# Twelve pairs of seven-product tiles: weight sums on VectorE instead of GpSimd, first products copied ahead of rounding, and half a values tile inside the last mLSTM unit

## The chip, the cores and the metric

One core of a Trainium2 chip runs the whole program. The metric is device time in microseconds (us) of one execution; smaller is better. The engines that matter here are TensorE (PE in the profile; its weight loads are PEld), VectorE (DVE), ScalarE (ACT), GpSimd (POOL) and SyncE (SP), which issues the loads.

## The reference

One layer of a trunk, for 128 context tokens and 512 latent tokens (640 columns in all) of width 1024:

```python
h = rms_norm(x, n_pre[0]) * (1 + sc0) + sh0
x = x + 0.5 * g0 * rms_norm(swiglu(h, f_in[0], f_out[0]), n_post[0])     # FFN 0, D_FF = 2816
h = rms_norm(x, n_pre[1]) * (1 + sc1) + sh1
y, st = token_mixer(h, *mix_w, ctx)          # mLSTM (8 heads) beside grouped attention (16 heads)
x = x + g1 * rms_norm(y, n_post[1])
h = rms_norm(x, n_pre[2]) * (1 + sc2) + sh2
x = x + 0.5 * g2 * rms_norm(swiglu(h, f_in[1], f_out[1]), n_post[2])     # FFN 1

def swiglu(h, w_in, w_out):
    a, b = jnp.split(h @ w_in, 2, axis=-1)
    return (jax.nn.silu(a) * b) @ w_out
```

## The kernel before

**Products in three passes.** Everything lies transposed, features on the 128 partitions and the 640 tokens along a row. Each float32 operand is split into a rounded high part and a low remainder, and a product is three matmuls: high by high, high by low, low by high. A weight tile (128 output features, 1024 inputs) is loaded into one of four buffers `raw`. ScalarE rounds it into `whi`, VectorE subtracts and leaves `wlo`, and TensorE then runs 8 blocks of inputs by 2 halves of 320 columns by 3 passes, 48 matmuls (`project`, L646 to L648).

**FFN 1 with seven products.** The inner features of an FFN are done in three phases of 8, 8 and 6. In phase 1 of the second FFN all 8 gate and up tile pairs, and in phase 2 the first 4, go through `seven`: Strassen's scheme in Winograd's form on 2 x 2 blocks. The blocks of weights are the two halves of the inputs of the gate tile (`gt`) and of the up tile (`ut`); the blocks of tokens are the two halves of 320 columns. Seven products of 4 input blocks by 3 passes, 12 matmuls each, take the place of eight. I call a pair g (0 to 11; n is its number in its phase) and its products M0 to M6 (the code's `i`). They go into three banks of PSUM, A B A C B C B in this order, so that a bank is written again before the pair is over, and its content has to be taken away first:

- M2 overwrites M0 in bank A: ScalarE first copies it to `kept_p1` (L1252).
- M4 overwrites M1 in bank B: VectorE first makes `sum_u2` from it (L1865).
- M5 overwrites M3 in bank C: ScalarE first copies it to `kept_p5` (L1261).
- M6 overwrites M4 in bank B: VectorE first makes `sum_u3` (L1875).

Each product needs its own weights: M0, M2 and M6 take half a tile as loaded, and M1, M3, M4 and M5 take one of the sums `w_sum` 1, 0, 2 and 3, 128 x 512 each. ScalarE rounds each (`prod_high`, L1233, which I call H0 to H6), VectorE leaves the remainder (`prod_low`, L1833, L0 to L6), and both go into a ring of four half buffers, so that H of one product waits for the product four before it. GpSimd makes the four sums of a pair during the pair before it (`weight_sums`, L1782 to L1791).

At the end of the pair VectorE adds the up half and multiplies it by the gate after Silu (`pair_product`, L1845 and L1849); ScalarE rounds this into `g_hi` (L1244), and VectorE leaves `g_lo` (L1853). Both do so during the next pair. Silu itself is done in two halves on ScalarE: left (L1257) after VectorE's L1869, and right (L1270) after VectorE's L1888.

Every engine runs its instructions in the order of the code and stops at a wait until the semaphore is reached; nothing overtakes it. On ScalarE the order in a pair is H3, `g_hi` of the pair before, `kept_p1`, H4, H5, H6, Silu left, `kept_p5`, H0 and H1 of the next pair, Silu right, H2 of the next pair.

**mLSTM units.** After the state updates there are 20 units (`UNITS`). For each unit n TensorE makes the numerators (`nums_of`, L1003 and L1006) in banks 0 and 1, from which VectorE makes the outputs (L2379 to L2393), ScalarE the root mean square (L1577 to L1582), VectorE scales (L2398), TensorE turns the result (`turn_hm`, L1014) and ScalarE stores it (L1591). `nums_of(n)` waits until VectorE has read the banks for unit n - 1 (L2388). Between the small products of the units, halves of gate projection tiles (`half_gemm`, 24 matmuls each) are laid as filler. The last unit has none: its numerators follow on `turn_hm(17)`, then `turn_hm(18)`, then the whole tile of the values projection `gemm(L_AV)`, then `turn_hm(19)`.

Of the kernel before, what the change touches and what calls it, by code (L numbers as in the profile page):

```python
# [47 lines left out]
RAWS = 4  # L48
# [86 lines left out]
def build(nc, a):  # L135
    ctx = ExitStack()
    with ctx:
# [466 lines left out]
        def _(pe):  # L604
            mm, tp = pe.matmul, pe.transpose

            def seven(g, n, base):
                gt, ut = pair_tiles(base, n)
                for i in range(7):
                    if i < 5:  # L610
                        pe.wait_ge(prod_lo, KEEP + 5 * g + i + 1)
                    else:
                        pe.wait_ge(raw_free, (gt, ut)[i - 5].n + 1 + RAWS)
                    if i == 0:
                        pe.wait_ge(ev[ut.slot], ut.pair - 1)
                    if i == 1 and g == 0:
                        pe.wait_ge(tok_lo, KEEP + 4)
                    if i == 2:
                        pe.wait_ge(act_kept, KEEP + 4 * g + 1)
                    if i == 4:  # L620
                        pe.wait_ge(dve_sums, KEEP + 6 * g + 1)
                    if i == 5:
                        pe.wait_ge(act_kept, KEEP + 4 * g + 3)
                    if i == 6:
                        pe.wait_ge(dve_sums, KEEP + 6 * g + 3)
                    out = psum[:, pair_banks(n)[(0, 1, 0, 2, 1, 2, 1)[i]], 0:HALF]
                    (wh, wl), (th, tl) = product(g, i), of_tokens(i)
                    for k in range(KH):
                        mm(out, wh[:, k, :], th[:, k, :], start=(k == 0), stop=False)  # L629
                        mm(out, wh[:, k, :], tl[:, k, :], start=False, stop=False)  # L630
                        last = mm(out, wl[:, k, :], th[:, k, :], start=False, stop=(k == KH - 1))  # L631
                    last.then_inc(prod_done if i < 5 else tile_done, 1)
# [387 lines left out]
            for n in range(UNITS):  # L1020
                if n + 1 < UNITS:
                    half_gemm(10 + 2 * n)
                    spread_m(n + 1)
                    front_of(n + 1)
                    half_gemm(11 + 2 * n)
                nums_of(n)
                if n >= 1:
                    turn_hm(n - 1)
            gemm(L_AV)
            turn_hm(UNITS - 1)  # L1030

            def qk_stats(n):
# [177 lines left out]
        def _(act):  # L1210
# [24 lines left out]
            def seven(g, n, base, last, first_g):  # L1235
                gt, ut = pair_tiles(base, n)
                s = gt.c // 2 % 2
                bank_a, _, bank_c = (psum[:, b, 0:HALF] for b in pair_banks(n))
                left, right = HCOLS

                def pair_high(m, before):
                    up = pair_tiles(base, m)[1]
                    act.wait_ge(ev[up.slot], up.pair + 1)
                    copy(g_hi[:, m, :], sb[before][:, :]).then_inc(g_hi_s, 1)  # L1244

                prod_high(g, 3, n, base)
                if n:
                    pair_high(n - 1, 1 - s)
                act.wait_ge(prod_done, KEEP + 5 * g + 1)
                if g:  # L1250
                    act.wait_ge(dve_sums, KEEP + 6 * (g - 1) + 2)
                copy(kept_p1, bank_a).then_inc(act_kept, 1)  # L1252
                prod_high(g, 4, n, base)
                prod_high(g, 5, n, base)
                prod_high(g, 6, n, base)
                act.wait_ge(dve_sums, KEEP + 6 * g + 2)
                fn(sa[s][:, left], sa[s][:, left], ACT.Silu).then_inc(act_kept, 1)  # L1257
                act.wait_ge(prod_done, KEEP + 5 * g + 4)
                if g:
                    act.wait_ge(dve_sums, KEEP + 6 * (g - 1) + 5)  # L1260
                copy(kept_p5, bank_c).then_inc(act_kept, 1)  # L1261
                if not last:
                    prod_high(g + 1, 0, n + 1, base)
                    prod_high(g + 1, 1, n + 1, base)
                else:
                    t = Tile(base + 2 * n + 2)
                    act.wait_ge(prod_done, KEEP + 5 * g + 5)
                    split(t, None, 0, first_g)
                act.wait_ge(dve_sums, KEEP + 6 * g + 6)
                fn(sa[s][:, right], sa[s][:, right], ACT.Silu).then_inc(act_kept, 1)  # L1270
                if not last:
                    prod_high(g + 1, 2, n + 1, base)
                else:
                    split(Tile(base + 2 * n + 3), None, ut.n + 3, first_g)
                    pair_high(n, s)

# [459 lines left out]
        def _(pool):  # L1736
# [34 lines left out]
                step(8, t4, of_h(h_hi, down, left), t2[:, :, :], sub)  # L1771
                step(9, t4, of_h(h_lo, down, left), t4[:, :, :], ALU.add)

            def weight_sums(g, n, base):
                gt, ut = pair_tiles(base, n)
                a1, a2 = raw[gt.raw], raw[ut.raw]
                sub = ALU.subtract
                for t in (gt, ut):
                    pool.wait_ge(raw_in[t.raw], 16 * (t.quad + 1))
                if g:  # L1780
                    pool.wait_ge(prod_lo, KEEP + 5 * (g - 1) + 4)
                pool.tensor_tensor(w_sum[0][:, :, :], a2[:, 0:KH, :], a2[:, KH:KC, :], ALU.add).then_inc(w_sum_in, 1)  # L1782
                pool.wait_ge(w_sum_in, KEEP + 4 * g + 1)
                pool.tensor_tensor(w_sum[1][:, :, :], w_sum[0][:, :, :], a1[:, 0:KH, :], sub).then_inc(w_sum_in, 1)
                if g:
                    pool.wait_ge(prod_lo, KEEP + 5 * (g - 1) + 5)
                pool.tensor_tensor(w_sum[2][:, :, :], a1[:, 0:KH, :], a2[:, 0:KH, :], sub).then_inc(w_sum_in, 1)
                if n:
                    pool.wait_ge(raw_free, pair_tiles(base, n - 1)[0].n + 1 + RAWS)
                pool.wait_ge(w_sum_in, KEEP + 4 * g + 2)  # L1790
                pool.tensor_tensor(w_sum[3][:, :, :], a1[:, KH:KC, :], w_sum[1][:, :, :], sub).then_inc(w_sum_in, 1)  # L1791

            for l in range(3):
                if l == 2:
                    token_sums()
                    base = T_FFN1
                    for p, nj in enumerate(PHASES):
                        for n in range(SEVEN[p]):
                            weight_sums(SEVEN_FROM[p] + n, n, base)
                        base += 2 * nj + KC  # L1800
                if l == 0:
                    pool.wait_ge(h_rdy, KC)
                elif l == 1:
                    pool.wait_ge(yl, KC)
                else:
                    pool.wait_ge(h_rdy, KC + n_half(l - 1, 1, KC - 1))
                for h in range(2):
                    for i in range(1, KC - 1):
                        add_y_square(l, i, h)

        @block.vector
        def _(dve):
# [13 lines left out]
            def prod_low(g, i, n, base):  # L1826
                gt, ut = pair_tiles(base, n)
                if i < 5:
                    dve.wait_ge(prod_hi, KEEP + 5 * g + i + 1)
                else:  # L1830
                    dve.wait_ge(w_hi, (gt, ut)[i - 5].n + 1)
                hi, lo = product(g, i)
                tt(lo, of_weights(i, gt, ut), hi.bitcast(F32), ALU.subtract).then_inc(prod_lo if i < 5 else raw_free, 1)  # L1833

            def seven(g, n, base, last, first_g, first_j):
                gt, ut = pair_tiles(base, n)
# [32 lines left out]
                tt(sa[s][:, left], bank_a, kept_p1, ALU.add).then_inc(dve_sums, 1)  # L1869
                prod_low(g, 6, n, base)  # L1870
                if not last:
                    prod_low(g + 1, 0, n + 1, base)
                dve.wait_ge(prod_done, KEEP + 5 * g + 5)
                dve.wait_ge(dve_sums, KEEP + 6 * g + 1)
                tt(sum_u3, bank_b, sum_u2, ALU.add).then_inc(dve_sums, 1)  # L1875
                dve.wait_ge(act_kept, KEEP + 4 * g + 3)
                dve.wait_ge(dve_sums, KEEP + 6 * g + 3)
                if n >= 2:
                    dve.wait_ge(g_lo_s, first_j + n - 1)
# [8 lines left out]
                tt(sa[s][:, right], bank_c, sa[s][:, right], ALU.add).then_inc(dve_sums, 1)  # L1888
                if not last:
                    prod_low(g + 1, 2, n + 1, base)  # L1890
                else:
                    pair_product(n, s)
                    pair_low(n, s)
# [234 lines left out]
            def ffn(f, base):  # L2128
                it = j0 = 0
                for p, nj in enumerate(PHASES):  # L2130
# [60 lines left out]
                    elif f == 1:  # L2191
                        for m in range(KC):
                            t = Tile(base + m)
                            if m < KC - 2:
                                split(t.plus(2))
                            if m == KC - 2:
                                prod_low(SEVEN_FROM[p + 1], 0, 0, base + KC)
                                prod_low(SEVEN_FROM[p + 1], 1, 0, base + KC)
                            elif m == KC - 1:
                                prod_low(SEVEN_FROM[p + 1], 2, 0, base + KC)  # L2200
                            elif p == 0 and m < 4:
                                token_low(m)
# [472 lines left out]
```

## Time and profile before

| | before |
|---|---|
| median of 3 runs | 1824.18 us (1822.89 to 1825.48) |
| profiled execution | 1820.2 us, span 1818.3 us |
| PE busy | 1757.6 us, 97% of the span |
| DVE busy | 1061.5 us, 58% |
| ACT busy | 705.7 us, 39% |
| POOL busy | 139.1 us, 8% |

The profiled execution is 4.0 us shorter than the median, and 1.9 us longer than its span. In the profile "busy" is time in which an engine executes; matmuls are pipelined and overlap each other, so PE's stalls are seen best as jumps in the start times of its matmuls. In a timeline the first number is the start, the second the duration, and square brackets hold the idle time before an instruction and what ended it.

### The profile page before, as it was taken

Reading aid. Unit: us, or ns where it says so; the run is one execution under the profiler, and the core shown is the slowest. Engines: PE = TensorE matmul, PEld = TensorE weight load, DVE = VectorE, ACT = ScalarE, POOL = GpSimd, SP = SyncE. Lnnn points to the kernel's source line nnn. Section 1 sums busy time; section 2 is a strip of 40 time slices with the busy share of each in tenths; the row PEclk is TensorE's granted clock in tenths of the full one; section 3 lists DMA queues with packets and bytes.
Section 4 is the critical chain, followed back from the end, with each engine's and each line's share of the span. In section 5 each row is a group of like instructions: output and inputs, shape, how many; then the busy total and the mean of one; then the engine's idle time right before and its main releaser. Section 6 shows DMA issues by size and latency. Waiting matters only on the chain. (4 is left out here: it accounts for less than half of the span.)

```text
span 1818.3 us, 30972 instructions
## 1 busy us (share of the span) xinstructions
PE 1757.6 (97%) x12434; PEld 1677.3 (92%) x12434; DVE 1061.5 (58%) x1819; ACT 705.7 (39%) x1262; POOL 139.1 (8%) x98
## 2 busy tenths in 40 slices
PE   5999999999999999999999999989999999999998
PEld 3999999999988998999999888889989999899897
DVE  4767566766467324555537877755364337863844
ACT  4432222212454322443445555544652234432444
POOL 0000000000110000000000000000207013312201
PEclk9999999999999999999999999999999999999999
DMA  9344443443304224323243211113232221221231
GB/s 377 123 145 135 154 150 127 161 136 106 105 4 151 71 70 100 89 89 94 77 132 110 81 39 39 39 43 130 68 107 79 70 80 55 84 85 60 90 128 58
DMA packets 53016, 183.74 MB, mean 101 GB/s; under 512 B 8593, under 2 KB 11299, under 8 KB 51875
## 3 DMA queue, kind: packets, MB, share of 16 engines
q1 hardware_dynamic: 52899, 182.10, 30.9%
q8 instruction: 83, 1.36, 0.3%
q14 instruction: 34, 0.28, 0.0%
HBM read 164.90 MB, written 16.52 MB: 100 GB/s over the span
## 5 line engine op out<-in xcount | busy, mean ns | idle before, releaser
L646 PE MATMUL psum<-h_hi,whi 128*128 128x320 f32 x1712 | 537.3, 314 | 0.2 <-ACT gate L1565 0.2
L648 PE MATMUL psum<-h_hi,wlo 128*128 128x320 f32 x1712 | 529.8, 309 | 0.0
L647 PE MATMUL psum<-h_lo,whi 128*128 128x320 f32 x1712 | 529.5, 309 | 0.0
L1824 DVE TENSOR_TENSOR wlo<-raw,whi 128x1024 fp32r<-128x1024 f32 x167 | 209.7, 1257 | 443.2 <-ACT whi L1216 443.2
L646 PEld LDWEIGHTS psum<-h_hi,whi 128*128 128x128 f32 x1712 | 322.0, 188 | 6.1 <-issue 1.9
L647 PEld LDWEIGHTS psum<-h_lo,whi 128*128 128x128 f32 x1712 | 322.2, 188 | 1.1
L648 PEld LDWEIGHTS psum<-h_hi,wlo 128*128 128x128 f32 x1712 | 321.9, 188 | 0.0
L1216 ACT CAST whi<-raw 128x1024 fp32r<-128x1024 f32 x167 | 173.9, 1042 | 241.6 <-PE psum L648 224.6
L647 PE MATMUL psum<-g_lo,whi 128*128 128x320 f32 x512 | 158.2, 309 | 0.0
L646 PE MATMUL psum<-g_hi,whi 128*128 128x320 f32 x512 | 158.2, 309 | 0.0
L648 PE MATMUL psum<-g_hi,wlo 128*128 128x320 f32 x512 | 158.2, 309 | 0.0
L2045 DVE SCALAR_TENSOR_TENSOR macc<-mw,silc,macc 128x512 f32<-128x512 f32 x196 | 133.3, 744 | 0.0
L1741 POOL TENSOR_TENSOR rb<-sq,sq 128x320 f32<-128x320 f32 (+2 forms) x6 | 6.3, 1050 | 1314.2 <-ACT sq L1306 1314.2
L646 PEld LDWEIGHTS psum<-g_hi,whi 128*128 128x128 f32 x512 | 96.1, 188 | 0.5
L647 PEld LDWEIGHTS psum<-g_lo,whi 128*128 128x128 f32 x512 | 96.1, 188 | 0.2
L648 PEld LDWEIGHTS psum<-g_hi,wlo 128*128 128x128 f32 x512 | 96.1, 188 | 0.0
L2467 DVE TENSOR_REDUCE amax<-psum 128x1 f32<-128x640 f32 x64 | 49.7, 819 | 7.3 <-PE psum L1089 7.3
L1460 ACT CAST g_hi<-sb 128x640 f32 (+1 forms) x32 | 23.3, 728 | 77.9 <-DVE sb L2150 77.9
L1675 ACT ACTIVATE sa<-psum,amax 128x640 f32<-128x640 f32 x64 | 50.5, 799 | 3.7 <-DVE amax L2467 3.7
L1449 ACT ACTIVATE sa<-psum 128x640 f32<-128x640 f32 x32 | 22.5, 703 | 73.8 <-PE psum L648 72.1
L2156 DVE TENSOR_TENSOR g_lo<-sb,g_hi 128x640 f32 (+1 forms) x32 | 29.5, 922 | 30.4 <-ACT g_hi L1460 30.4
L1169 PE MATMUL psum<-a_hi,whi 128*128 128x320 f32 x128 | 42.3, 331 | 0.2 <-DVE a_lo L2425 0.2
(409 smaller groups left out, 3464.6 us busy)
## 6 DMA issues: line engine op xcount, KB each, us to landing
raw<-in_w_ffn_in SPq DMA_DIRECT2D x88, 512.0 KB, 3.6
raw<-in_w_mix SPq DMA_DIRECT2D x77, 512.0 KB, 4.1
mw<-in_w_mod SPq DMA_DIRECT2D x28, 768.0 KB, 5.0
raw<-in_w_ffn_out SPq DMA_DIRECT2D x32, 512.0 KB, 3.5
mw<-in_w_mod SPq DMA_DIRECT2D x4, 2048.0 KB, 18.2
gate<-gate_keep SPq DMA_DIRECT2D x24, 320.0 KB, 4.5
mw<-in_w_mod SPq DMA_DIRECT2D x14, 512.0 KB, 4.2
gate_keep<-gate SPq DMA_DIRECT2D x20, 320.0 KB, 4.7
```

Source lines behind the costliest of these rows:

```text
L646: mm(out, whi[t.slot][:, k, :], hi[:, k, cols], start=(k == 0), stop=False)
L647: mm(out, whi[t.slot][:, k, :], lo[:, k, cols], start=False, stop=False)
L648: last = mm(out, wlo[t.slot][:, k, :], hi[:, k, cols], start=False, stop=(k == nk - 1))
L1169: mm(out, whi[t.slot][:, k, :], a_hi[:, k, cols], start=(k == 0), stop=False)
L1216: copy((to or whi[t.slot])[:, 0:nk, :], raw[t.raw][:, 0:nk, :]).then_inc(w_hi, 1)
L1449: fn(halves(sa[s][:, :]), both(t.bank), ACT.Silu).then_inc(ev[t.slot], 1)
L1460: copy(out, sb[s][:, :]).then_inc(g_hi_s, 1)
L1675: last = fn(sa[s][:, :], flat(s)[:, 0:N], ACT.Exp, bias=amax[:, s:s + 1], accum_out=asum[:, s:s + 1])
L1824: tt(lo[:, 0:nk, :], raw[t.raw][:, 0:nk, :], hi[:, 0:nk, :].bitcast(F32), ALU.subtract).then_inc(raw_free, 1)
L2045: last = stt(acc, w[:, k, :], by, acc, ALU.mult, ALU.add)
L2156: tt(g_lo[:, jj, :].rearrange("p o n -> p (o n)"), sb[s][:, :], g_hi[:, jj, :].rearrange("p o n -> p (o n)").bitcast(F32), ALU.subtract).t ...
L2467: dve.tensor_reduce(amax[:, s:s + 1], flat(s)[:, 0:N], AX.X, ALU.max, negate=True).then_inc(nmx, 1)
```

## The change

- The four sums of each of the 12 pairs are made by VectorE (new function `weight_sum`), and not by GpSimd. Sums 0 and 1 stand behind L6 of the pair before, sum 2 behind L0, sum 3 behind L2. For the first pair of a phase they stand among the last two tiles of the phase before.
- On ScalarE `kept_p1` moves ahead of the rounding of `g_hi`, `kept_p5` moves ahead of the left Silu, and H2 of the next pair moves ahead of the right Silu. The counts of two waits follow.
- `gemm(L_AV)` is cut in two halves: one ahead of the numerators of unit 19, the other where the whole stood, behind `turn_hm(18)`.

```diff
@@ tensor, seven
                     if i == 5:
-                        pe.wait_ge(act_kept, KEEP + 4 * g + 3)
+                        pe.wait_ge(act_kept, KEEP + 4 * g + 2)
@@ tensor, mLSTM units
                     half_gemm(11 + 2 * n)
+                else:
+                    half_gemm(2 * (L_AV - L_MO))
                 nums_of(n)
                 if n >= 1:
                     turn_hm(n - 1)
-            gemm(L_AV)
+            half_gemm(2 * (L_AV - L_MO) + 1)
             turn_hm(UNITS - 1)
@@ scalar, seven
                 prod_high(g, 3, n, base)
-                if n:
-                    pair_high(n - 1, 1 - s)
                 act.wait_ge(prod_done, KEEP + 5 * g + 1)
                 if g:
                     act.wait_ge(dve_sums, KEEP + 6 * (g - 1) + 2)
                 copy(kept_p1, bank_a).then_inc(act_kept, 1)
+                if n:
+                    pair_high(n - 1, 1 - s)
                 prod_high(g, 4, n, base)
                 prod_high(g, 5, n, base)
                 prod_high(g, 6, n, base)
-                act.wait_ge(dve_sums, KEEP + 6 * g + 2)
-                fn(sa[s][:, left], sa[s][:, left], ACT.Silu).then_inc(act_kept, 1)
                 act.wait_ge(prod_done, KEEP + 5 * g + 4)
                 if g:
                     act.wait_ge(dve_sums, KEEP + 6 * (g - 1) + 5)
                 copy(kept_p5, bank_c).then_inc(act_kept, 1)
+                act.wait_ge(dve_sums, KEEP + 6 * g + 2)
+                fn(sa[s][:, left], sa[s][:, left], ACT.Silu).then_inc(act_kept, 1)
...
+                if not last:
+                    prod_high(g + 1, 2, n + 1, base)
                 act.wait_ge(dve_sums, KEEP + 6 * g + 6)
                 fn(sa[s][:, right], sa[s][:, right], ACT.Silu).then_inc(act_kept, 1)
-                if not last:
-                    prod_high(g + 1, 2, n + 1, base)
-                else:
+                if last:
@@ gpsimd: weight_sums and its calls are removed
-                pool.tensor_tensor(w_sum[0][:, :, :], a2[:, 0:KH, :], a2[:, KH:KC, :], ALU.add).then_inc(w_sum_in, 1)
...
@@ vector
+            def weight_sum(g, n, base, j):
+                gt, ut = pair_tiles(base, n)
+                a1, a2 = raw[gt.raw], raw[ut.raw]
+                up, down = slice(0, KH), slice(KH, KC)
+                if j == 0:
+                    for t in (gt, ut):
+                        dve.wait_ge(raw_in[t.raw], 16 * (t.quad + 1))
+                if j in (1, 3):
+                    dve.wait_ge(w_sum_in, KEEP + 4 * g + (j + 1) // 2)
+                if g and j < 3:
+                    dve.wait_ge(prod_lo, KEEP + 5 * (g - 1) + (4, 2, 5)[j])
+                elif g:
+                    dve.wait_ge(raw_free, (pair_tiles(base, n - 1) if n else pair_tiles(base - KC, 0))[0].n + 1 + RAWS)
+                one, two = ((a2[:, up, :], a2[:, down, :]), (w_sum[0][:, :, :], a1[:, up, :]), (a1[:, up, :], a2[:, up, :]),
+                            (a1[:, down, :], w_sum[1][:, :, :]))[j]
+                tt(w_sum[j][:, :, :], one, two, ALU.subtract if j else ALU.add).then_inc(w_sum_in, 1)
@@ vector, seven
                 prod_low(g, 6, n, base)
                 if not last:
+                    weight_sum(g + 1, n + 1, base, 0)
+                    weight_sum(g + 1, n + 1, base, 1)
                     prod_low(g + 1, 0, n + 1, base)
+                    weight_sum(g + 1, n + 1, base, 2)
...
                 if not last:
                     prod_low(g + 1, 2, n + 1, base)
+                    weight_sum(g + 1, n + 1, base, 3)
@@ vector, last two tiles of a phase
+                                weight_sum(SEVEN_FROM[p + 1], 0, base + KC, 0)
+                                weight_sum(SEVEN_FROM[p + 1], 0, base + KC, 1)
                                 prod_low(SEVEN_FROM[p + 1], 0, 0, base + KC)
                                 prod_low(SEVEN_FROM[p + 1], 1, 0, base + KC)
                             elif m == KC - 1:
+                                weight_sum(SEVEN_FROM[p + 1], 0, base + KC, 2)
+                                weight_sum(SEVEN_FROM[p + 1], 0, base + KC, 3)
                                 prod_low(SEVEN_FROM[p + 1], 2, 0, base + KC)
```

On VectorE, in the second half of pair 1, the kernel before has L6 of this pair, L0 of pair 2, the three sums from PSUM, L1, the last sum and L2 (`wlo_71`, `wlo_72`, `whi_69` and `whi_70` are the halves of the ring, `sq_78` holds `sum_u2` and `sum_u3`):

```order
L1833 TENSOR_TENSOR wlo_72<-raw_65,wlo_72 128x512
L1833 TENSOR_TENSOR whi_69<-raw_66,whi_69 128x512
L1875 TENSOR_TENSOR sq_78<-psum,sq_78 128x320
L1880 TENSOR_TENSOR sb_76<-sq_78,sq_77 128x320
L1881 TENSOR_TENSOR sa_74<-sq_78,sq_77 128x320
L1833 TENSOR_TENSOR wlo_71<-w_sum_146,wlo_71 128x512
L1888 TENSOR_TENSOR sa_74<-psum,sa_74 128x320
L1833 TENSOR_TENSOR whi_70<-raw_66,whi_70 128x512
```

In the changed kernel the same place reads:

```order
L1811 TENSOR_TENSOR wlo_72<-raw_65,wlo_72 128x512
L1828 TENSOR_TENSOR w_sum_145<-raw_67 128x512
L1828 TENSOR_TENSOR w_sum_146<-w_sum_145,raw_66 128x512
L1811 TENSOR_TENSOR whi_69<-raw_66,whi_69 128x512
L1828 TENSOR_TENSOR w_sum_147<-raw_66,raw_67 128x512
L1873 TENSOR_TENSOR sq_78<-psum,sq_78 128x320
L1878 TENSOR_TENSOR sb_76<-sq_78,sq_77 128x320
L1879 TENSOR_TENSOR sa_74<-sq_78,sq_77 128x320
L1811 TENSOR_TENSOR wlo_71<-w_sum_146,wlo_71 128x512
L1886 TENSOR_TENSOR sa_74<-psum,sa_74 128x320
L1811 TENSOR_TENSOR whi_70<-raw_66,whi_70 128x512
L1828 TENSOR_TENSOR w_sum_148<-raw_66,w_sum_146 128x512
```

Three of the four sums now stand ahead of `sum_u3` (L1875, now L1873), for which M6 waits, and the fourth ahead of the next pair's `pair_product`.

On ScalarE, from H3 of pair 1 to H2 of pair 2, the kernel before has:

```order
L1233 CAST whi_69<-w_sum_145 128x512
L1244 CAST g_hi<-sb_75 128x640
L1252 COPY sq_77<-psum 128x320
L1233 CAST wlo_71<-w_sum_147 128x512
L1233 CAST whi_70<-w_sum_148 128x512
L1233 CAST wlo_72<-raw_65 128x512
L1257 ACTIVATE sa_74<-sa_74 128x320
L1261 COPY sq_77<-psum 128x320
L1233 CAST whi_69<-raw_66 128x512
L1233 CAST wlo_71<-w_sum_146 128x512
L1270 ACTIVATE sa_74<-sa_74 128x320
L1233 CAST whi_70<-raw_66 128x512
```

and the changed kernel:

```order
L1235 CAST whi_69<-w_sum_145 128x512
L1252 COPY sq_77<-psum 128x320
L1246 CAST g_hi<-sb_75 128x640
L1235 CAST wlo_71<-w_sum_147 128x512
L1235 CAST whi_70<-w_sum_148 128x512
L1235 CAST wlo_72<-raw_65 128x512
L1261 COPY sq_77<-psum 128x320
L1263 ACTIVATE sa_74<-sa_74 128x320
L1235 CAST whi_69<-raw_66 128x512
L1235 CAST wlo_71<-w_sum_146 128x512
L1235 CAST whi_70<-raw_66 128x512
L1274 ACTIVATE sa_74<-sa_74 128x320
```

Both copies from PSUM moved ahead of the instruction that reads a result of VectorE, and so did H2 ahead of the right Silu.

## Rows read from the trace of the kernel before

**Rows 1.** The page: busy time of each engine, and TensorE's granted clock.

```profile
PE 1757.6 (97%) x12434; PEld 1677.3 (92%) x12434; DVE 1061.5 (58%) x1819; ACT 705.7 (39%) x1262; POOL 139.1 (8%) x98
...
PEclk9999999999999999999999999999999999999999
```

**Rows 2.** Windows, the eight pairs of phase 1: busy us (instructions), clock, DMA share.

```profile
1505.00:1616.00 111.00, 102.72 (x672) 98.28 (x672) 95.00 (x122) 48.15 (x94) 39.96 (x28) 1.00 0.25 75
```

**Rows 3.** Waits of TensorE, 1495 to 1735 us: total, times, longest.

```profile
PE psum L629 <- ACT sq L1261: 5.9, 8, 0.7
PE psum L629 <- ACT sq L1252: 5.5, 10, 0.6
```

**Rows 4.** Timeline of TensorE, pair 2: first matmuls of M2, M4, M5, next M2.

```profile
1537.75 0.38 PE L629 MATMUL psum<-h_hi,whi 128*128 128x320 f32 x1 [0.55 <-ACT sq L1252]
...
1541.51 0.38 PE L629 MATMUL psum<-t_hi,whi 128*128 128x320 f32 x1
...
1544.25 0.38 PE L629 MATMUL psum<-h_hi,wlo 128*128 128x320 f32 x1 [0.75 <-ACT sq L1261]
...
1552.06 0.39 PE L629 MATMUL psum<-h_hi,wlo 128*128 128x320 f32 x1 [0.54 <-ACT sq L1252]
```

**Rows 5.** Timeline of ScalarE, pair 2.

```profile
1536.55 0.73 ACT L1244 CAST g_hi<-sb 128x640 fp32r<-128x640 f32 x1 [1.55 <-DVE sb L1849]
1537.19 0.42 ACT L1252 COPY sq<-psum 128x320 f32<-128x320 f32 x1
1537.50 0.62 ACT L1233 CAST whi<-w_sum 128x512 fp32r<-128x512 f32 x1
...
1543.32 0.47 ACT L1257 ACTIVATE sa<-sa 128x320 f32<-128x320 f32 x1 [2.92 <-DVE sa L1869]
1543.69 0.41 ACT L1261 COPY sq<-psum 128x320 f32<-128x320 f32 x1
```

**Rows 6.** Timeline of VectorE, pair 2.

```profile
1535.70 0.82 DVE L1849 TENSOR_TENSOR sb<-sb,sa 128x640 f32<-128x640 f32 x1
...
1537.31 1.94 DVE L1853 TENSOR_TENSOR g_lo<-sb,g_hi 128x640 fp32r<-128x640 f32 x1 [0.19 <-ACT g_hi L1244]
1539.18 1.78 DVE L1833 TENSOR_TENSOR whi<-w_sum,whi 128x512 fp32r<-128x512 f32 x1
1540.88 0.48 DVE L1865 TENSOR_TENSOR sq<-psum,sq 128x320 f32<-128x320 f32 x1
...
1544.71 0.68 DVE L1833 TENSOR_TENSOR wlo<-raw,wlo 128x512 fp32r<-128x512 f32 x1
1545.31 0.48 DVE L1875 TENSOR_TENSOR sq<-psum,sq 128x320 f32<-128x320 f32 x1
```

**Rows 7.** Timeline of GpSimd, pair 2: sum 0 for pair 3.

```profile
1537.29 1.28 POOL L1782 TENSOR_TENSOR w_sum<-raw 128x512 f32<-128x512 f32 x1 [7.38 <-DVE wlo L1833]
```

**Rows 8.** Timelines of VectorE, ScalarE and TensorE in pair 7, without GpSimd.

```profile
1609.69 0.69 DVE L1833 TENSOR_TENSOR wlo<-w_sum,wlo 128x512 fp32r<-128x512 f32 x1
...
1613.07 0.43 ACT L1261 COPY sq<-psum 128x320 f32<-128x320 f32 x1 [0.76 <-PE psum L631]
...
1611.11 0.31 PE L629 MATMUL psum<-t_hi,whi 128*128 128x320 f32 x1
...
1618.15 0.31 PE L646 MATMUL psum<-g_hi,whi 128*128 128x320 f32 x1
```

**Rows 9.** Timeline of TensorE around the last mLSTM unit, filler left out.

```profile
905.91 0.61 PE L1003 MATMUL psum<-vt,sa 128*128 128x129 f32 x4
...
907.64 0.38 PE L1014 MATMUL psum<-cst,hmt 128*128 128x128 f32 x2
910.41 0.68 PE L1003 MATMUL psum<-vt,sa 128*128 128x129 f32 x4 [2.39 <-DVE sb L2388]
...
912.67 0.41 PE L1014 MATMUL psum<-cst,hmt 128*128 128x128 f32 x2 [0.29 <-ACT hm L1591]
```

**Rows 10.** Timeline of ScalarE there: the store that `turn_hm(19)` waits for.

```profile
915.43 0.61 ACT L1591 ACTIVATE hm<-psum,vT 128x128 f32<-128x128 f32 x2
```

More of the change, by code:

```diff
@@ L1772, in token_sums @@
                 step(9, t4, of_h(h_lo, down, left), t4[:, :, :], ALU.add)
[L1774 to L1781, printed above, removed]
-                pool.tensor_tensor(w_sum[0][:, :, :], a2[:, 0:KH, :], a2[:, KH:KC, :], ALU.add).then_inc(w_sum_in, 1)
[L1783 to L1791, printed above, removed]
             for l in range(3):
@@ L1795, in _ @@
                     token_sums()
[L1796 to L1800, printed above, removed]
                 if l == 0:
@@ L1875, in seven @@
                 tt(sum_u3, bank_b, sum_u2, ALU.add).then_inc(dve_sums, 1)
-                dve.wait_ge(act_kept, KEEP + 4 * g + 3)
+                dve.wait_ge(act_kept, KEEP + 4 * g + 2)
                 dve.wait_ge(dve_sums, KEEP + 6 * g + 3)
```

## The prediction

> **What bounds the kernel now.** I read the page first: TensorE is busy 97% of the span at the full clock, the higher of its two levels (2.4 GHz), and no other engine is above 58% [rows 1]. So only time in which TensorE stands still can be won, or be added. The windows over phase 1 then show that this average hides something: there VectorE is busy 95.0 of 111 us, and TensorE only 102.7 [rows 2]. The view of TensorE's waits names two places in the pairs: M2 waits for `kept_p1` ten times, 5.5 us, and M5 for `kept_p5` eight times, 5.9 us [rows 3]. This leaves out part of the loss, so I took it from the start times. From one M2 to the next, 1537.75 to 1552.06, a pair takes 14.31 us [rows 4]. Without stalls four products take 1618.15 - 1611.11 = 7.04 us [rows 8], one 1.76 us (a matmul starts each 0.147 us), and seven 12.32 us. **A pair loses 1.99 us.** M2 to M4 is 3.76 us where 3.52 are needed, and M4 to M5 2.74 where 1.76 are [rows 4]: about 0.2 at M4, 1.0 at M5, and the 0.8 that are left at M2.
>
> Who is late? *M2:* `kept_p1` starts at 1537.19, right behind `g_hi`, which waited until 1536.55 for VectorE's product [rows 5, 6]. M2 was about 0.7 late, so M0 had begun at 1537.75 - 0.7 - 3.52 = 1533.5 and was done by 1535.5 (a product is done 1.96 us after its start, 1611.11 to 1613.07 [rows 8]). The copy stood behind another's wait. *M4:* `sum_u2` ends at 1541.36 and M4 starts 0.15 later [rows 4, 6]; ahead of it VectorE spent 1.94 us on `g_lo` and 1.78 on L4. *M5:* `kept_p5` stands behind the left Silu, and this waited 2.92 us for VectorE [rows 5]. So both late things on VectorE go back to its long instructions. They lie beside GpSimd's sums (1.28 us for sum 0 from 1537.29 [rows 7]); L4 in pair 7, which has no sums beside it, takes 0.69 us, and M5 doesn't stall there: `kept_p5` starts 1.96 us behind M3 [rows 8]. *Last mLSTM unit:* TensorE stands 2.39 us ahead of the numerators of unit 19 and 0.29 us ahead of `turn_hm(18)` [rows 9].
>
> The Trainium skill (GPSIMD Engine Reference, Specifications) says that GpSimd shares its interfaces to SBUF with VectorE and that instructions of VectorE with two SBUF inputs suffer from it. By that rule the stretched rows shrink once GpSimd is silent; the trace agrees, 1.78 us beside it and 0.69 without.
>
> **The change, part by part.**
>
> *ScalarE's order, M2.* `kept_p1` needs H3 and M0 alone. With M0 started at 0, it runs from 1.96 to 2.38 (0.42 [rows 5]), and M2, due at 3.52, can start from 2.53 on. The stall goes, with 1.0 us to spare.
>
> *VectorE's sums.* No row shows one of these on VectorE. The nearest is L4 or L6: same shape, two SBUF inputs, 0.68 us, and the next instruction starts 0.60 us behind it [rows 6]; the farthest is GpSimd's own 1.28 us [rows 7]. I see no reason for less than 0.60. I take 0.60, and 0.79 where the next reads the result (sum 0 into sum 1, 0.69 + 0.10): 2.6 us a pair. What falls away is 1.94 - 0.82 = 1.1 us at `g_lo` (0.82 is the row of the same length, L1849 [rows 6]) and 1.78 - 0.69 = 1.1 at L4. So VectorE's load stays about what it was, even if no other instruction is relieved.
>
> *One pair as a timetable*, us from the start of M0, product i due at 1.76 i. H6 needs M2 (done 5.48), ends at 6.10; L6 starts 6.14, sum 0 6.74, sum 1 7.53, and L0 could start at 8.13. ScalarE: `kept_p5` at 7.24 (M3 done), Silu 0.31 later (the start to start of rows 5) at 7.55, H0 0.37 later at 7.92, ended at 8.54. L0 8.58, sum 2 9.18, `sum_u3` 9.78 to 10.26, M6 free at 10.41, **due at 10.56: 0.15 us to spare**, the tightest place. `kept_p5` ends at 7.65, M5 is due at 8.80. Then the two sums into `sb` and `sa` 10.36 and 10.77, L1 11.18, L1888 (now L1886) 11.78, L2 12.18 (H2 runs at 10.76, when M5 is done), sum 3 12.78. `pair_product` starts at 13.38, that is 1.06 into the next pair; its multiplication ends at 2.46, `g_hi` 2.50 to 3.23, H4 to 3.75, L3 2.38, `g_lo` 3.27, L4 4.01, `sum_u2` 4.61 to 5.09 (M4 due 7.04), L5 5.02, the left sum 5.62, and L6 waits for H6 again at 6.14. The timetable closes: VectorE's twenty instructions fill about 11.6 of 12.32 us, and no product is late.
>
> *Sum for the pairs.* Eight pairs lose 1.99 us, two more (7 and 11, the last of a phase) only M2's 0.8: 15.9 + 1.6 = **17.5 us**, all of it won.
>
> *What else the edit touches.* H2 ahead of the right Silu delays this by nothing: H2 is done at 11.38, its input only at 12.26. The first sums of a phase stand in tiles of 7.04 us in which VectorE has at most four such instructions and one addition, 3.4 us. The loads of a pair start when the pair two before it frees the buffers, a whole pair ahead; GpSimd waited for VectorE and not for a load [rows 7], and VectorE's sum 0 comes later than GpSimd's did. If that cover were gone, each late us would be one on M0. SP and GpSimd have nothing else queued here.
>
> *mLSTM.* Half a tile, 24 matmuls, is 3.52 us; it is put into a wait of 2.39, whose end (VectorE's reading of the banks) doesn't move. The numerators take 2.26 us to `turn_hm(18)` and take 1.73 in the unit before [rows 9]: 2.39 + 0.53 = 2.92 us to win. But `turn_hm(19)` has now only half a tile ahead of it. The store that it needs ends at 915.43 + 0.61 = 916.04 [rows 10], 5.63 behind the numerators' start, 5.8 with the handover; TensorE gets there at 1.73 + 0.3 (the two transposes) + 3.52 = 5.55. It waits 0.25. **Won: 2.7 us** (bounds 1.9, if another 0.8 is late in that chain, and 2.9).
>
> Total 17.5 + 2.7 = 20.2; with 0.2 for stray handovers 20.0. Profiled execution: 1820.2 - 20.0 = 1800.2 (span 1798.3). The median of the runs stands 4.0 above it: **1804.2 us**. A measurement of this kernel can tell 0.2%, 3.6 us, from no change.
>
> **The rivals.**
>
> *A. M6 waits for `sum_u3`.* The margin is 0.15 us over a chain of six instructions on two engines. If the sums and their neighbours take 0.3 more in all, M6 starts 0.15 late and 0.07 go in getting started again (at M4 about 0.2 are lost for a sum that ended 0.15 before). For: ten of twelve pairs hold the chain. Against: each term has its row. 0.2 to 0.5 us by 10: 1806 to 1809. 12%.
>
> *B. VectorE becomes the bound.* If its instructions couldn't start before the one ahead has ended, seven L and four sums by 0.69, the addition, multiplication and `g_lo` by 0.5 + 0.8 + 0.8, six small ones by 0.48 and handovers make about 12.8 us, more than 12.32, and with its waits up to 13.3: 0.5 to 1.0 by 10, 1809 to 1814. Against: L6 starts at 1544.71 for 0.68, and the next at 1545.31, 0.08 before its end [rows 6]. The Trainium skill (VectorE: DVE Perf Modes, The DRAIN you can't avoid) has the next operation wait until the pipeline is empty, which would be this rival; the row speaks against it. 5%.
>
> *C. Slower than before: the sums are dear on VectorE.* Without them its load is 9.0 us a pair, with t each 9.0 + 4t. The change pays until this passes 14.31 + 0.27 (the mLSTM gain spread over ten pairs): t = 1.40. At 1.78, as L4 had beside GpSimd [rows 6], a pair takes 16.1, and the time is 1824.2 + 17.9 - 2.7 = 1839. It would need something else to hold VectorE back as GpSimd did; none is seen in pair 7 [rows 8]. 3%.
>
> *D. The copies stay late.* `kept_p5` still stands behind H6, and the sums might keep VectorE from feeding it. If M5's stall stays, 8 by 1.0: 1812. The timetable has 1.0 us of room there. 4%.
>
> **How the numbers follow.** Forecast 76% (its own range 1802 to 1807, from 0.1 us a pair of unseen stalls and the mLSTM bounds), A 12, B 5, C 3, D 4. The range 1801 to 1809 takes in the forecast's and A, 8 to 9 in 10; with sums of 1.28 us on VectorE, the far bound, `sum_u3` would be 1.5 late and the time near 1821, which is between B and C. Faster by over 0.2%: forecast, A, B, D and little else, 95%; within 0.2% 2%, slower 3%.
>
> **What would show it.** In the changed trace: pairs 12.3 us from M2 to M2; no rows of TensorE waiting for L1252 or L1261; sums at 0.69 us and L4 and `g_lo` at 0.69 and 0.82; `sum_u3` ending at about 10.3 in the pair. The numerators of unit 19 without idle time, `turn_hm(19)` with about 0.25. A pair of 12.4 to 12.8 with idle ahead of M6 is A; 12.8 to 13.3 with VectorE never idle is B; above 14.3, C. The prediction is wrong if the other stages, which the edit leaves alone, shift by more than a us.

## The result and the profile after

| | before | after |
|---|---|---|
| median of 4 runs | 1823.54 us (1822.82 to 1825.48) | 1801.36 us (1799.59 to 1802.42) |
| profiled execution | 1820.2 us, span 1818.3 | 1801.4 us, span 1799.5 |
| phase 1, eight pairs | 111.28 us | 98.56 us |
| phase 2, four pairs | 54.19 us | 49.28 us |

The change is faster, ratio 0.9878 (95% interval 0.9864 to 0.9891): 22.2 us by the medians, 18.8 by the profiled executions. The last two rows are from the start times of TensorE's matmuls, from the first of a phase's pairs to the first behind them.

The page of the changed kernel, its first line (beside [rows 1]):

```profile
PE 1753.2 (97%) x12434; PEld 1679.4 (93%) x12434; DVE 1053.5 (59%) x1867; ACT 709.2 (39%) x1262; POOL 69.1 (4%) x50
```

The shares hardly move, though 1.2% of the time is gone. VectorE has 48 instructions more and is busy 8 us less; GpSimd is busy 70 us less. The windows show it where it happens (columns as in [rows 2]: TensorE, its loads, VectorE, ScalarE, GpSimd, then clock, DMA share, GB/s):

```profile
1505.00:1604.00 99.00, 99.00 (x677) 99.00 (x676) 87.33 (x152) 50.73 (x94) 0.00 (x0) 1.00 0.27 86
```

TensorE is busy the whole window. The timeline of TensorE in pair 2, first matmul of M2 here and in the pair behind (beside the first and last of [rows 4]):

```profile
1533.92 0.31 PE L629 MATMUL psum<-h_hi,whi 128*128 128x320 f32 x1
...
1546.24 0.31 PE L629 MATMUL psum<-h_hi,wlo 128*128 128x320 f32 x1
```

The two M2 start 12.32 us apart, with no idle time in brackets; between 1490 and 1725 us TensorE has no wait at all. ScalarE there (beside [rows 5]):

```profile
1532.36 0.43 ACT L1252 COPY sq<-psum 128x320 f32<-128x320 f32 x1 [0.99 <-PE psum L631]
1532.90 0.73 ACT L1246 CAST g_hi<-sb 128x640 fp32r<-128x640 f32 x1
...
1537.64 0.43 ACT L1261 COPY sq<-psum 128x320 f32<-128x320 f32 x1 [1.14 <-PE psum L631]
1537.96 0.47 ACT L1263 ACTIVATE sa<-sa 128x320 f32<-128x320 f32 x1
```

Both copies now wait for TensorE's product, which is what they read. VectorE (beside [rows 6]):

```profile
1533.67 0.83 DVE L1848 TENSOR_TENSOR g_lo<-sb,g_hi 128x640 fp32r<-128x640 f32 x1 [0.19 <-ACT g_hi L1246]
1534.41 0.68 DVE L1811 TENSOR_TENSOR whi<-w_sum,whi 128x512 fp32r<-128x512 f32 x1
...
1539.59 0.68 DVE L1828 TENSOR_TENSOR w_sum<-raw,raw 128x512 f32<-128x512 f32 x1
1540.19 0.48 DVE L1873 TENSOR_TENSOR sq<-psum,sq 128x320 f32<-128x320 f32 x1
```

`g_lo` took 1.94 us and takes 0.83, L4 took 1.78 and takes 0.68. The pair's M0 starts at 1533.92 - 3.52 = 1530.40, so `sum_u3` ends at 10.27 in the pair (the timetable had 10.26). With the handover of 0.15 M6 could start at 10.42; it is due at 10.56, so 0.14 us are left. TensorE around the last mLSTM unit (beside [rows 9]):

```profile
906.04 0.61 PE L1003 MATMUL psum<-vt,sa 128*128 128x129 f32 x4
...
907.77 0.38 PE L1014 MATMUL psum<-cst,hmt 128*128 128x128 f32 x2
911.51 0.61 PE L1003 MATMUL psum<-vt,sa 128*128 128x129 f32 x4
...
913.24 0.38 PE L1014 MATMUL psum<-cst,hmt 128*128 128x128 f32 x2
917.21 0.41 PE L1014 MATMUL psum<-cst,hmt 128*128 128x128 f32 x2
```

From the numerators of unit 18 to the last transposes it is 11.17 us; before it was 14.05 (905.91 to 919.96). Between 913.24 and 917.21 lie 3.97 us, 0.2 more than two transposes (0.25) and half a tile (3.52): the last transposes wait 0.2 us.

**The ledger of the two profiled executions**, changed less before, in us. Start to the numerators of unit 18: +0.1. From these to the last transposes: -2.9. From there to the first pair: +1.6. Phase 1: -12.7. Phase 2: -4.9. The rest within 0.1. The sum is -18.8. The +1.6 lies in stages that the edit leaves alone, and the prediction had named a shift of more than 1 us there as a sign that it is wrong. Its cause is TensorE's clock, and it lies in the trace of before. The windows of the kernel before, and of the changed one, at the start of the attention sweep:

```profile
1010.00:1035.00 25.00, 21.82 (x188) 19.44 (x186) 22.10 (x47) 15.69 (x30) 0.00 (x0) 1.00 0.26 91
```

```profile
1010.00:1035.00 25.00, 21.97 (x187) 19.58 (x185) 20.77 (x43) 14.04 (x27) 0.00 (x0) 0.93 0.14 50
```

In the changed kernel's trace 7% of that window's clock is missing, that is 3.4 us at the lower level (1.2 GHz), which cost up to 1.7 us; in the trace of before it stays at the higher one. Three more executions of the kernel before (experiment 9) have 0.93 there like the changed kernel, and take 588.36 to 588.45 us for the stretch; the changed kernel takes 588.55, and the first trace of before took 586.91. So the edit did not cause the +1.6.

### The profile page after: what moved, and what is told of

Same layout as the page of the kernel before. It is cut to its first block, busy times and chain, and to the rows that moved or that the text cites. A ratio compares the mean times of both kernels' runs of the same rounds, so it can differ in the third digit from the quotient of the medians.

```text
span 1799.5 us, 30985 instructions
## 1 busy us (share of the span) xinstructions
PE 1753.2 (97%) x12434; PEld 1679.4 (93%) x12434; DVE 1053.5 (59%) x1867; ACT 709.2 (39%) x1262; POOL 69.1 (4%) x50
## 4 chain that ended last, share of the span: by engine, by line
PE 91%; DVE 5%; ACT 2%; issue 1%; DMA 1%; SPq 0%; DVEq 0%; ACTq 0%
PE psum L646 19%; PE psum L647 19%; PE psum L648 19%; PE psum L631 3%; PE psum L629 3%; PE psum L630 3%; PE psum L686 2%; PE psum L688 2%; PE psum L687 2%; PE psum L1123 2%; PE psum L1113 2%; PE psum L1088 2%; PE psum L1003 1%; DMA mw<-in_w_mod 1%; PE psum L1172 1%
## 5 line engine op out<-in xcount | busy, mean ns | idle before, releaser
L1113 PE MATMUL psum<-cst,sa 128*128 128x128 f32 x336 | 43.2, 277 | 0.0
```

The source lines that it names most:

```text
L1113: last = tp(turned(s, b), sa[s][:, b * P:(b + 1) * P], ident)
```

## The experiments

Each of the first eight was timed against the kernel before on the same chip, in five rounds. Experiments 1 to 4 ran on one chip, 5 to 8 on a second. A difference "by the trace" is taken from the start times in single profiled executions.

**1. The values tile alone.** The kernel before with this edit:

```diff
+                else:
+                    half_gemm(2 * (L_AV - L_MO))
                 nums_of(n)
...
-            gemm(L_AV)
+            half_gemm(2 * (L_AV - L_MO) + 1)
```

> The kernel before with one edit: the values tile cut in two around the last mLSTM unit. Theory (the filler hides the 2.39 us wait for VectorE's reading of the banks, and turn_hm(19) now waits about 0.25): 2.7 to 2.9 us faster than before, ratio 0.9985; in the trace no idle time ahead of the numerators of unit 19, and nothing of it given back in the attention stage. Rival (the gain is lost again between this unit and the FFN, as the ledger of the changed kernel's trace shows 1.6 us less than was won): 1.2 us, ratio 0.9993, with the loss at the same place in every profile whatever the granted clock there.

Measured: ratio 0.9973 (0.9961 to 0.9985), 4.9 us. That is neither the wait alone (2.8) nor the rival's 1.2. The 2.39 us wait is gone from the trace, where the stretch from the numerators of unit 18 to the last transposes takes 11.17 us as in the changed kernel, and the pairs take what they did (111.31 and 54.21 us). Experiment 9 looks for the rest.

**2. The sums alone.** VectorE makes the weight sums; ScalarE's order is the old one:

```diff
-            def weight_sums(g, n, base):
...
+            def weight_sum(g, n, base, j):
...
+                    weight_sum(g + 1, n + 1, base, 0)
...
```

> The kernel before with the weight sums on VectorE alone; ScalarE's order and the values tile as before. Theory (kept_p1 stands behind g_hi, which hangs on VectorE's product, and VectorE comes to it later, since H2 is behind the right Silu and sum 3 is ahead of the product): M4's and M5's stalls go, M2's grows from 0.8 to about 1.0, a pair takes 13.35 us, and the time falls by about 7 us (ratio 0.996). Rival (the sums on VectorE are most of the gain): 12 us or more. Second rival (VectorE too full without the new order): no gain, M2 stalls 2 us.

Measured: ratio 0.9952 (0.9939 to 0.9964), 8.8 us; by the trace the pairs won 7.4 us (105.73 and 52.37). TensorE's waits between 1490 and 1740 us:

```profile
PE psum L629 <- ACT sq L1252: 7.9, 10, 0.8
```

Only M2 stalls, and longer than before (0.8 us for 0.6 in [rows 3]); from one M2 to the next it is 13.34 us (13.35 were expected). On ScalarE the copy still stands right behind `g_hi`, which waits for VectorE:

```profile
1542.76 0.73 ACT L1244 CAST g_hi<-sb 128x640 fp32r<-128x640 f32 x1 [2.16 <-DVE sb L1842]
1543.39 0.42 ACT L1252 COPY sq<-psum 128x320 f32<-128x320 f32 x1
```

So the sums on VectorE free M4 and M5, and leave M2 to the order.

**3. The order alone.** ScalarE's new order, GpSimd's sums:

```diff
-                        pe.wait_ge(act_kept, KEEP + 4 * g + 3)
+                        pe.wait_ge(act_kept, KEEP + 4 * g + 2)
...
-                if n:
-                    pair_high(n - 1, 1 - s)
                 act.wait_ge(prod_done, KEEP + 5 * g + 1)
...
                 copy(kept_p1, bank_a).then_inc(act_kept, 1)
+                if n:
+                    pair_high(n - 1, 1 - s)
```

> The kernel before with ScalarE's new order alone (both copies ahead, H2 ahead of the right Silu); the weight sums stay on GpSimd. Theory (copies no longer hang on VectorE, so M2's and M5's stalls go, but VectorE's instructions stay stretched beside GpSimd's: start to start they add up to 13.1 us a pair): pairs of 13.1 to 13.3 us, now bound by VectorE, about 10 us faster (ratio 0.9945), TensorE waiting for VectorE's rows instead of ScalarE's. Rival (the order alone was the fault): pairs of 12.4 us, 17 us faster.

Measured: ratio 0.9957 (0.9941 to 0.9972), 7.8 us; by the trace the pairs won 10.5 us (103.84 and 51.18), as the theory said. The waits:

```profile
PE psum L629 <- DVE sq L1875: 5.2, 8, 0.7
```

ScalarE is out of the list and VectorE's `sum_u3` has come into it: M2's, M4's and M5's stalls are gone, and M6 has a new one. The runs show less than the trace, 7.8 us, because TensorE's clock was lower in this kernel's executions: 0.9895 in the mean of six, against 0.9912 in the 13 of the kernel before beside it. At 1.8 us for 0.001 (last section) that is an estimated 3 us.

**4. The pairs without the values tile.** The changed kernel with this edit:

```diff
-                else:
-                    half_gemm(2 * (L_AV - L_MO))
                 nums_of(n)
...
-            half_gemm(2 * (L_AV - L_MO) + 1)
+            gemm(L_AV)
```

> The changed kernel with the values tile whole again behind unit 19, so that only the pairs are changed. Theory: the pairs' own ledger, 17.6 us faster than before (ratio 0.9904), pairs of 12.32 us; the changed kernel is 2.7 to 2.9 faster than this one. Rival (the two parts overlap or the mLSTM part is worth nothing in time): as fast as the changed kernel, ratio 0.988.

Measured: ratio 0.9908 (0.989 to 0.9927), 16.8 us; pairs 98.56 and 49.28 us, as in the changed kernel. Together with experiment 1 this is 21.7 of the 22.2 us: the two parts add up, within intervals of 2 us and more on each. Sums and order nearly add up too, by the trace: 7.4 + 10.5 = 17.9 apart, 17.6 together. That is a coincidence. Either edit alone removes M4's and M5's stalls, which counts them twice, and each leaves a new loss (M2 stalls 0.2 longer with the sums alone, M6 stalls with the order alone), which the two together don't have.

**5. One more instruction ahead of `sum_u3`.** The changed kernel, in ten pairs:

```diff
                     weight_sum(g + 1, n + 1, base, 2)
+                    tt(rb[:, 0:KH * P], cst[:, 0:KH * P], cst[:, P:5 * P], ALU.subtract)
```

> The changed kernel with one more VectorE instruction of 128 x 512 (two SBUF inputs, its result goes into a free buffer and is used by nothing) in each of the ten pairs that make sums, directly ahead of sum_u3, for which M6 waits. Theory (the timetable's margin there is 0.15 us, and the trace shows 0.14): M6 starts 0.46 late, 0.07 more for getting started, ten times: 5 us slower than the changed kernel, pairs of 12.85 us, TensorE waiting for VectorE's sum_u3. Rival (the margin is larger than the timetable says, VectorE catches up): no difference. Second rival (VectorE is close to its bound anyway, so any added instruction costs its 0.6 us): 6 us, wherever it stands.

Measured: 1808.19 us (ratio 0.99, 0.9877 to 0.9923); by the trace the pairs take 102.29 and 50.88 us, 5.3 more than the changed kernel's. By the runs it is 4.9 us more than experiment 6, which has the same instruction elsewhere. The waits:

```profile
PE psum L629 <- DVE sq L1874: 3.0, 10, 0.3
```

Ten waits for `sum_u3`, at the expected place and size: the margin is 0.14 us, not more.

**6. The same instruction behind `sum_u3`.**

```diff
                 tt(sa[s][:, right], sum_u2, kept_p5, ALU.add).then_inc(dve_sums, 1)
                 if not last:
+                    tt(rb[:, 0:KH * P], cst[:, 0:KH * P], cst[:, P:5 * P], ALU.subtract)
```

> The changed kernel with the same additional instruction in the same ten pairs, but behind sum_u3 and its two followers. Theory (only what stands between H0 and sum_u3 is tight; VectorE's load of 11.6 + 0.6 still fits into 12.32 us, and sum_u2 has 1.8 us to spare): no difference to the changed kernel, pairs of 12.32 us. Second rival of the run before (VectorE is at its bound): 6 us slower, as there.

Measured: ratio 0.9878 (0.9855 to 0.99), the changed kernel's own; pairs 98.56 and 49.28 us, to the hundredth. So where an instruction stands decides whether it costs anything, and VectorE is not at its bound.

**7. GpSimd active beside VectorE.** The changed kernel, with four instructions of GpSimd a pair that do nothing for the result:

```diff
+                for count in (4, 4, 5, 5):
+                    if g:
+                        pool.wait_ge(prod_lo, KEEP + 5 * (g - 1) + count)
+                    ghost[0] += 1
+                    pool.tensor_tensor(rb[:, 0:KH * P], cst[:, 0:KH * P], cst[:, P:5 * P], ALU.subtract).then_inc(tok_sum, 1)
+                    pool.wait_ge(tok_sum, KEEP + 10 + ghost[0])
```

> The changed kernel, VectorE making the sums, and GpSimd executing four instructions of the same shape a pair as well, at the places where it made the sums before; their results go into a free buffer and are used by nothing. Theory (two engines with two SBUF inputs each stretch one another): VectorE's instructions beside them take 1.6 to 1.9 us instead of 0.69, its load rises from 11.6 to over 15 us a pair, and the kernel is slower than before the change, 1825 to 1840 us. Rival (what VectorE was stretched by was only a wait for what GpSimd made, not GpSimd's activity): no difference to the changed kernel.

Measured: 1835.05 us, 32 us more than experiment 6 and slower than before the change (ratio 1.0055, 1.0036 to 1.0075). The timelines of GpSimd, VectorE and TensorE in one pair:

```profile
1538.65 3.14 POOL L1786 TENSOR_TENSOR rb<-cst 128x512 f32<-128x512 f32 x2 [9.15 <-DVE wlo L1829]
...
1539.31 1.32 DVE L1866 TENSOR_TENSOR g_lo<-sb,g_hi 128x640 fp32r<-128x640 f32 x1 [0.83 <-ACT g_hi L1246]
1540.56 1.79 DVE L1829 TENSOR_TENSOR whi<-w_sum,whi 128x512 fp32r<-128x512 f32 x1
...
1544.26 0.48 DVE L1882 TENSOR_TENSOR sa<-psum,sq 128x320 f32<-128x320 f32 x1
...
1549.11 0.39 PE L629 MATMUL psum<-t_hi,whi 128*128 128x320 f32 x1 [2.12 <-DVE sq L1891]
```

L4 is back at 1.79 us, though nothing reads what GpSimd makes: its activity stretches VectorE. The left sum at 1544.26, which has one of its inputs in PSUM, keeps its 0.48 us while GpSimd executes (1542.49 to 1545.49). A pair takes 15.7 us (`pair_product` from 1537.05 to 1552.80), and the eight and four pairs 121.31 and 59.47 us.

Not all of this is VectorE. TensorE waits ten times for `sum_u3` in this trace, and its clock falls behind some of the waits. Windows that start shortly ahead of a wait's end, a wait of 1.66 us (it ends at 1564.87) and one of 2.12 (it ends at 1549.11):

```profile
1562.00:1572.00 10.00, 8.34 (x58) 8.11 (x57) 9.60 (x16) 4.32 (x8) 1.92 (x2) 1.00 0.26 95
1547.00:1557.00 10.00, 7.89 (x43) 7.92 (x44) 8.46 (x15) 4.42 (x8) 2.52 (x2) 0.83 0.21 67
```

The six waits of 2.11 to 2.46 us have 0.83 behind them, which is 3.4 us at the lower level each; the four of 1.49 to 1.66 us have 1.00. Six such stretches cost up to 10 us (6 x 1.7) of the 33 by which the pairs are longer than in the changed kernel.

**8. The last transposes later.** An attempt to cover the 0.2 us that are left:

```diff
             half_gemm(2 * (L_AV - L_MO) + 1)
+            pe.wait_ge(den_s, 4 * UNITS)
+            half_gemm(2 * (L_AV - L_MO) + 2)
             turn_hm(UNITS - 1)
...
-                if l > L_AV:
+                if l == L_AV + 1:
+                    half_gemm(2 * (L_AV - L_MO) + 3)
+                elif l > L_AV:
```

> The changed kernel with turn_hm(19) behind the first half of the next values tile instead of ahead of it, so that its 0.3 us wait is covered. Theory: 0.3 us faster than the changed kernel, which no measurement of this size can tell; in the trace no idle time ahead of the last transposes. Its use is a second look at the changed kernel's time and clock, since nothing else differs: 1801 us. Rival (the later store delays the loads of the attention stage): TensorE waits for a load there, 1 us or more slower.

Measured: 1802.5 us, ratio 0.9873 (0.985 to 0.9896): no difference that can be told. In the trace the transposes start 7.26 us behind those before them, which is a whole tile (7.04) and the two transposes ahead of it, so the wait is covered, and no load was late. But a wait of 0.6 us that the changed kernel has not (L1058, for VectorE's `av`) has come behind them, and from the numerators of unit 18 to the first pair it is 600.15 us where the changed kernel takes 599.72. The wait was moved, not won.

**9. The clock at the last mLSTM unit.** In experiment 1 something besides the wait was won. The traces that kept the wait (2, 3 and 4) had a granted clock of 0.91, 0.83 and 0.91 between 905 and 925 us; the changed kernel and experiments 1 and 5 to 8 have 1.00. But so had the first trace of the kernel before. So the kernel before was profiled in three more executions, on a third chip:

> The kernel before, looked at again for TensorE's granted clock between 905 and 925 us. Theory (the 2.4 us in which TensorE stands at the last mLSTM unit often lead to a stretch at the lower clock level, which is what the values tile's half wins beyond the wait itself): a window below 1.00 there, as in the three traces so far that keep the wait and differ from this kernel elsewhere (0.91, 0.83, 0.91), though the first trace of this kernel had 1.00. Rival (the low stretches fall anywhere and the three were chance): 1.00 there.

> The same look again, with the same expectations: theory a granted clock below 1.00 between 905 and 925 us, rival 1.00.

> The same look a third time, with the same expectations: theory a granted clock below 1.00 between 905 and 925 us, rival 1.00.

The windows of the three:

```profile
905.00:925.00 20.00, 17.47 (x118) 16.50 (x117) 6.91 (x18) 7.23 (x22) 0.00 (x0) 0.91 0.17 44
```

```profile
905.00:925.00 20.00, 17.60 (x113) 16.39 (x112) 10.63 (x30) 7.60 (x28) 0.00 (x0) 0.83 0.31 86
```

```profile
905.00:925.00 20.00, 17.61 (x119) 16.69 (x118) 7.12 (x18) 7.40 (x23) 0.00 (x0) 0.91 0.15 44
```

and of experiment 1, where the half tile lies in the wait:

```profile
905.00:925.00 20.00, 19.92 (x147) 18.89 (x146) 9.77 (x26) 9.58 (x31) 0.00 (x0) 1.00 0.29 85
```

So with the wait 6 of 7 traces fall to the lower level (3.4 us of it at 0.91, 6.8 at 0.83), without it 0 of 6. The first trace of the kernel before, on which the prediction was built, was the one that did not. On the chip of experiments 1 to 4 alone it is 3 of 3 with the wait and 0 of 1 without.

What this is worth can be read from the start times, in us (experiment 8 is left out, since its transposes stand elsewhere):

| trace | numerators of unit 18 to last transposes | from there to the first pair |
|---|---|---|
| kernel before, first trace | 14.05 | 586.91 |
| kernel before again | 15.34, 16.34, 15.25 | 588.45, 588.44, 588.36 |
| experiments 2, 3, 4 (with the wait) | 15.22, 16.39, 15.15 | 588.34, 588.41, 588.34 |
| changed kernel, experiments 6, 7 | 11.17, 11.17, 11.17 | 588.55, 588.58, 588.55 |
| experiment 1 | 11.17 | 586.94 |
| experiment 5 | 11.17 | 589.90 |

In the first column a clock of 0.91 costs 1.1 to 1.3 us beyond the wait, and 0.83 costs 2.3. Over the seven traces with the wait the mean is 15.39 us, so the half tile wins 4.2 us there, 2.9 of them the wait and 1.3 the clock. In the second column the two traces near 586.9 are those whose clock was 1.00 between 1010 and 1035 us; the others had 0.93 there, with the wait and without it. Experiment 5 had another 3.4 us at the lower level later on.

## Why the prediction was right

**The pairs: right, in mechanism and size.** 17.5 us were forecast, 17.6 came (12.7 + 4.9). That M2 waited for a copy behind another's wait is shown by experiments 2 (M2's stall stays without the new order) and 3 (it goes with the order alone). That M4 and M5 hung on VectorE's instructions, and these on GpSimd's activity, is shown by experiment 2 (both stalls go) and 7 (the instructions are long again when GpSimd is active for nothing). Experiment 3 adds that the new order alone frees them too, with VectorE's instructions still stretched (in its trace L4 takes 1.78 us); the sums on VectorE are then what keeps M6 from stalling.

**The timetable: right to 0.01 us at its tightest place.** Start to start 0.60 us for a sum was the right row to take; the sums take 0.68 to 0.69. Sum 1 starts 0.72 us behind sum 0, whose result it reads, where 0.79 were taken; this changes nothing, since L0 behind it waits 0.42 us for H0. Experiment 5 puts in 0.60 and TensorE gives 5.3 us back, 0.53 a pair: 0.60 - 0.14, and 0.07 for getting started. Rival A was therefore the nearest: a little over 0.14 us more in that chain would have started it.

**Rival B fell with experiment 6:** with a twenty-first instruction in the pair VectorE still costs nothing. The rule of the Trainium skill (VectorE: DVE Perf Modes, The DRAIN you can't avoid) that the next operation doesn't start until the pipe empties, read as the price of each instruction, would have made this rival true, 5 to 10 us. The same paragraph excepts a next operation that is not held, and the traces show earlier starts: 0.60 us from start to start at 0.68 to 0.69 us of duration. **Rival C needed something that holds VectorE back.** Experiment 7 provides it, and the kernel is 9 us slower than the kernel before beside it, where the rival was priced at 15. That is not the rival's own mechanism: most of the sums stay at 0.68 to 0.69 us in it, what is stretched are the L instructions and `g_lo`, and up to 10 us are TensorE's clock. **Rival D** did not come; both copies wait for TensorE alone.

**The mLSTM term: the mechanism right, the size short.** 2.7 us were forecast for the wait; the two traces show 2.9, with the remaining 0.2 us at `turn_hm(19)` as worked out. The time of experiment 1 shows 4.9 (interval 2.7 to 7.1). The prediction had no term for the clock behind the wait, that is, it put it at nothing: the traces of experiment 9 show 1.3 us for it in the mean, 4.2 us in all. That the low stretch goes with the wait is shown, 6 of 7 against 0 of 6; the 4.2 are a mean over seven single executions, and the 0.7 us between 4.2 and 4.9 are inside the interval.

**The step from the profile to the median: the one that failed.** The forecast added 4.0 us to 1800.2, as if the median stood as far above the profiled execution in both kernels. It doesn't: before the change the profiled execution is 3.3 us below the median of the four runs, and after it (1801.4) it is at the median. The difference is for the most part low-clock stretches that the first trace was spared, one at the last unit and one between 1010 and 1035 us. Two of the three executions of the kernel before in experiment 9 have both stretches and take 1823.38 and 1823.82 us, 3.2 and 3.6 more than the first trace; 2.8 and 2.7 of that lie between the numerators of unit 18 and the first pair. The third, 1831.62 us, has lost another 7.5 us ahead of unit 18. The changed kernel keeps the second stretch and has lost the first together with the wait. So the one trace of before understates what the change wins, 18.8 us where the medians show 22.2.

**How near it was.** 1801.36 us is 2.8 below the forecast, below the forecast's own range (1802 to 1807) and only 0.4 inside the stated one (1801 to 1809); one of the four executions, 1799.59, lies outside it. The low end of 1801 had no reason of its own in the working, so it was in part luck that the result fell inside. The 17.5 us of the pairs owe nothing to it.

## What to carry to other kernels

A queue in order makes an instruction as late as the latest wait ahead of it: look at what stands ahead of the copy that frees a bank, and put it behind nothing but its own input. Moving work from an engine with time to spare (GpSimd, busy 8%) to a busier one can shorten the busier one, where the two hold each other up: VectorE got 48 instructions more and was busy 8 us less. Before trusting one trace's span against another's, compare the granted clock of the two window by window; and where a timetable from rows leaves a margin, one idle instruction ahead of and one behind the tight place tells whether it is real.

## What the runs showed of the hardware

- Instructions of VectorE with two inputs in SBUF take 1.3 to 1.9 us instead of 0.69 (128 x 512) or 0.83 (128 x 640) while GpSimd executes instructions with two inputs in SBUF, whether or not anything passes between them (experiment 7). The Trainium skill (GPSIMD Engine Reference, Specifications) states this contention; the traces agree.
- VectorE's instructions with one input in PSUM kept their 0.48 us beside the same GpSimd instructions (experiment 7).
- 2.4 us in which TensorE stood still at the last mLSTM unit were followed by 3.4 or 6.8 us at its lower clock level in 6 of 7 traces, and in none of 6 where work filled them. In the pairs of experiment 7 all six waits of 2.11 to 2.46 us were followed by 3.4 us at that level, and none of the four of 1.49 to 1.66 us. The stalls of 0.5 to 0.7 us, two to a pair, had a clock of 1.00 throughout [rows 2].
- Run to run the time of one kernel goes with the mean granted clock: the four executions of the changed kernel had 1799.59 us at 0.994, 1801.31 and 1801.41 at 0.993 and 1802.42 at 0.992. The 13 executions of the kernel before beside experiments 5 to 8 reach from 1819.67 us at 0.994 to 1832.13 at 0.987, which is 1.8 us for 0.001.
